# A mixture-of-experts loop whose sums stay in four PSUM banks, with expert weights loaded as half slabs

## The reference, cut to what matters

```
y = zeros(256, 1024)
for each block of tokens that chose the same expert e:
    xb    = the block's tokens
    y_blk = (silu(xb @ w_gate[e]) * (xb @ w_up[e])) @ w_down[e]
    y[token] += weight[token, e] * y_blk
x = x + gt2 * y
```

## Time and profile before

| what | value |
|---|---|
| timed runs, median of 3 | 3115.14 us |
| profiled execution, its own time | 3118.14 us |
| its span, first to last instruction | 3116.3 us |
| mean granted TensorE clock | 0.959 |
| TensorE / VectorE / ScalarE busy | 92% / 63% / 50% of the span |
| the loop over experts | from about 505 to 1379 us of the span |
| DMA in the loop | 345 GB/s mean between 600 and 1300 us |

### The profile page before, as it was taken

The page is one execution under the profiler, slowest core; times in us unless marked ns, Lnnn a source line. Parts: engine busy times, 40 slices in busy tenths (PEclk is TensorE's granted clock), DMA queues, the critical chain, the costliest instruction groups (busy, mean ns, idle before and its releaser), DMA issues.

```text
span 3116.3 us, 42400 instructions
## 1 busy us (share of the span) xinstructions
PE 2864.4 (92%) x15763; PEld 2357.9 (76%) x15763; DVE 1956.5 (63%) x2197; ACT 1550.4 (50%) x1558; POOL 183.6 (6%) x210
## 2 busy tenths in 40 slices
PE   7999998999899998979999999899999999998997
PEld 1476787667676766768898897789788988977996
DVE  1335667888888888874567436544545674375554
ACT  2143455777777777763444434434334454354342
POOL 0000000000000000000045000000000540000000
PEclk9989998999999999998998999999989999999999
DMA  7522436898989989873343005444433420154454
GB/s 301 189 81 81 182 135 257 342 351 332 356 337 361 349 331 348 338 289 115 136 143 128 1 4 220 176 169 175 178 112 136 159 109 1 36 203 160 176 190 169
DMA packets 57945, 612.11 MB, mean 196 GB/s; under 512 B 12641, under 2 KB 18337, under 8 KB 21442
## 3 DMA queue, kind: packets, MB, share of 16 engines
q1 hardware_dynamic: 57794, 610.04, 51.6%
HBM read 608.97 MB, written 1.05 MB: 196 GB/s over the span
## 4 chain that ended last, share of the span: by engine, by line
issue 47%; PE 27%; DVE 10%; DMA 6%; POOL 5%; ACT 4%; DVEq 0%; SPq 0%; POOLq 0%; ACTq 0%
DVE arena_rounded L1608 8%; DMA weight_slabs<-in_expert_slabs 5%; PE psum_vector L572 3%; ACT arena_rounded L1605 3%; PE psum_vector L517 2%; PE psum_vector L519 2%; PE psum_vector L518 2%; POOL arena L3183 2%; PE psum_scalar L517 2%; PE psum_vector L1654 2%; PE psum_scalar L518 2%; PE psum_scalar L519 2%; PE psum_vector L544 2%; POOL arena L3186 2%; PE psum_scalar L1641 2%
## 5 line engine op out<-in xcount | busy, mean ns | idle before, releaser
L2004 DVE TENSOR_TENSOR weight_slabs_rounded<-weight_slabs,arena_rounded 128x2048 fp32r<-128x2048 f32 x208 | 478.1, 2306 | 427.3 <-ACT arena_rounded L2001 410.4
L1608 DVE TENSOR_TENSOR arena_rounded<-weight_slabs,arena_rounded 128x2048 fp32r<-128x2048 f32 x290 | 651.5, 2287 | 64.2 <-ACT arena_rounded L1605 52.0
L2001 ACT ACTIVATE arena_rounded<-weight_slabs 128x2048 fp32r<-128x2048 f32 x208 | 396.1, 1912 | 454.7 <-PE psum_vector L519 261.9
L1605 ACT ACTIVATE arena_rounded<-weight_slabs 128x2048 fp32r<-128x2048 f32 x290 | 548.1, 1912 | 137.9 <-DMA weight_slabs<-in_expert_slabs 57.3
L517 PE MATMUL psum_vector<-arena_rounded,arena_rounded 128*128 128x512 f32 (+3 forms) x1312 | 480.2, 366 | 41.6 <-DVE weight_slabs_rounded L2004 31.0
L517 PE MATMUL psum_scalar<-arena_rounded,arena_rounded 128*128 128x256 f32 (+1 forms) x1456 | 477.8, 328 | 32.0 <-DVE weight_slabs_rounded L2004 17.3
L1641 PE MATMUL psum_scalar<-arena_rounded,arena_rounded 128*128 128x512 f32 x768 | 322.4, 420 | 72.8 <-DVE arena_rounded L1608 62.8
L519 PE MATMUL psum_vector<-arena_rounded,arena_rounded 128*128 128x512 f32 (+3 forms) x960 | 375.5, 391 | 0.0
L518 PE MATMUL psum_vector<-weight_slabs_rounded,arena_rounded 128*128 128x512 f32 x880 | 348.8, 396 | 0.0
L517 PEld LDWEIGHTS psum_scalar<-arena_rounded,arena_rounded 128*128 128x128 f32 x1456 | 285.0, 196 | 62.3 <-issue 12.5
L517 PEld LDWEIGHTS psum_vector<-arena_rounded,arena_rounded 128*128 128x128 f32 (+1 forms) x1312 | 256.6, 196 | 83.4 <-DVE weight_slabs_rounded L2004 41.1
(11 more groups left out here) (462 smaller groups left out, 4212.1 us busy)
## 6 DMA issues: line engine op xcount, KB each, us to landing
weight_slabs<-in_expert_slabs SPq DMA_DIRECT2D x145, 2048.0 KB, 9.2
weight_slabs<-in_layer_slabs SPq DMA_DIRECT2D x103, 2048.0 KB, 7.7
weight_slabs<-in_mixer_slabs SPq DMA_DIRECT2D x32, 2048.0 KB, 7.5
weight_slabs<-in_layer_slabs SPq DMA_DIRECT2D x6, 1024.0 KB, 5.5
arena<-in_mem SPq DMA_DIRECT2D x3, 1024.0 KB, 10.2
arena<-in_b_gate SPq DMA_DIRECT2D x6, 512.0 KB, 4.6
constants<-in_constants SPq DMA_DIRECT2D x1, 1025.0 KB, 5.2
arena<-in_x SPq DMA_DIRECT2D x1, 1024.0 KB, 7.5
```

The source lines that it names most:

```text
L1605: e.activation(high_, whole, ACT.Copy).then_inc(S("expert_high"), 1)
L1608: e.tensor_tensor(low, whole, high_.bitcast(F32), ALU.subtract).then_inc(S("expert_split"), 1)
L2001: e.activation(fr(high), low, ACT.Copy).then_inc(S("weights_high"), 1)
L2004: e.tensor_tensor(fr(low), low, fr(high).bitcast(F32), ALU.subtract).then_inc(S("weights_split"), 1)
```

## The change: what it does

The sums over the experts stay in PSUM: all four banks of `psv` accumulate through the whole loop, two tiles of 128 tokens by two sides of 512 columns. `combine` writes them with `start=False`. Ahead of the loop TensorE writes zeros there (4 fp32 matmuls with a zeroed `selwT`), behind a wait for the first gathered tokens (`xg_ready`). VectorE's `combined` goes, and at the end one instruction multiplies the four banks by `gt2`. The rings are remade: folds, gather and down sums share two banks (`psa` bank 2 and a new one in `pst`), the gate and up sums and the transposes the other two. A block takes 6 banks of the first ring: folds 0 and 1, gather, fold 2, two down sums. Expert slabs are loaded as halves of 1024 KB, each with its own semaphore count, and each as soon as the difference of the half before it in that place is done. GpSimd clears `selwT` earlier and `yacc` no more.

```
-MOE_V, MOE_A, MOE_STEP = 10, 7, 8
+MOE_V, MOE_A, MOE_STEP = 6, 7, 8
...
-        pst = ctx.enter_context(nc.psum_tensor("psum_tick", [P, 2], F32))
+        pst = ctx.enter_context(nc.psum_tensor("psum_tick", [P, BANK], F32))
+        moe_vector_banks, moe_scalar_banks = [psa[:, 2, :], pst[:, :]], [psa[:, 0, :], psa[:, 1, :]]
...
-            G = Banks(pe, psv, moe["vector_full"], moe["vector_free"])
+            G = Banks(pe, moe_vector_banks, moe["vector_full"], moe["vector_free"])
+            pe.wait_ge(m["scalar_free"], MIX_A + 3)
...
+            step(e.memset(selwT, 0.0))
+            e.sem_inc(S("set_for_products"), 1)
             e.wait_ge(S("blocks_known"), 1)
-            for sum_ in (yacc, ye, selwT):
-                step(e.memset(sum_, 0.0))
+            step(e.memset(ye, 0.0))
             e.sem_inc(S("ye_ready"), 1)
...
-                for n in slabs_:
-                    sp.wait_ge(S("expert_split"), 18 * i + 2 * n + 2)
-                    src = a["expert_slabs"][bass.ds(expert, 1), n, :, :].rearrange("e p n -> (e p) n")
-                    sp.dma_start(flat_slab(n % 3), src).then_inc(m[f"slab{n % 3}"], 16)
+                for h in halves_:
+                    sp.wait_ge(S("expert_split"), 18 * i + h + 1)
+                    src = a["expert_slabs"][bass.ds(expert, 1), h // 2, :, :].rearrange("e p n -> (e p) n")
+                    at = h % 2 * 4 * BANK
+                    sp.dma_start(expert_half(h)[0], src[:, at:at + 4 * BANK]).then_inc(half_arrived(h)[0], 16)
...
-            def combine(V):
+            def combine(last=False):
                 for t in range(NT):
-                    for half in range(2):
-                        V.close(pe.matmul(V.open(), selwT[:, t * P:(t + 1) * P], ye[:, half * BANK:(half + 1) * BANK],
-                                          start=True, stop=True))
+                    for side in range(2):
+                        mm = pe.matmul(psv[:, 2 * t + side, :], selwT[:, t * P:(t + 1) * P],
+                                       ye[:, side * BANK:(side + 1) * BANK], start=False, stop=last)
+                return mm
...
+            pe.wait_ge(S("set_for_products"), 2)
+            pe.wait_ge(S("xg_ready"), 1)
+            for bank in range(4):
+                pe.matmul(psv[:, bank, :], selwT[:, 0:P], cst[:, 0:BANK], start=True, stop=False)
             with pe.Fori(0, n_blocks) as i:
-                V = Banks(pe, psv, m["vector_full"], m["vector_free"], base=MOE_V * i + 1, looped=True)
-                A = Banks(pe, psa, m["scalar_full"], m["scalar_free"], base=MOE_A * i, looped=True)
+                V = Banks(pe, moe_vector_banks, m["vector_full"], m["vector_free"], base=MOE_V * i + 1, looped=True)
+                A = Banks(pe, moe_scalar_banks, m["scalar_full"], m["scalar_free"], base=MOE_A * i, looped=True)
...
-                combine(V)
+                combine()
...
-            def combined(V):
-                for t in range(NT):
-                    for half in range(2):
-                        cell = yacc[:, t, half * BANK:(half + 1) * BANK]
-                        V.give(tt(cell, cell, V.take(), ALU.add))
...
                 low_parts(2, 3, 4, 5, 6)
-                combined(V)
                 low_parts(7)
...
-            combined(V)
-            V.given()
             Splitter(e, 0, high=False).upto(1)
             step = Count(e, S("vector_between"))
-            step(tt(yacc, yacc, over(gt2, NT), ALU.mult))
+            e.wait_ge(m["vector_full"], MOE_V * n_blocks + 2)
+            step(tt(yacc, psv[:].rearrange("p (t b) n -> p t (b n)", b=2), over(gt2, NT), ALU.mult))
```

More of the change, by code:

```diff
@@ L191, in __init__ @@
         self.base, self.looped, self.n, self.closed = base, looped, 0, 0
-        self.size = psum.shape[1]
+        self.banks = psum if isinstance(psum, list) else [psum[:, k, :] for k in range(psum.shape[1])]
+        self.size = len(self.banks)
     def open(self, after=None):
@@ L203, in open @@
         self.n += 1
-        return self.psum[:, n % self.size, :]
+        return self.banks[n % self.size]
     def close(self, mm):
@@ L218, in take @@
         self.eng.wait_ge(self.full, self.base + self.n + 1)
-        return self.psum[:, self.n % self.size, :]
+        return self.banks[self.n % self.size]
     def give(self, ins, wait=False):
@@ L824, in pe_mixer @@
             used_now(mm)
[L825 removed]
+            pe.wait_ge(S("set_for_products"), 1)
             for n in range(2):
```

56 lines of the change are left out of this document (29 added, 27 removed).

## The result

The kernel after takes 3120.9 us (median of 20 runs) where the kernel before took 3115.6 us beside it: ratio 1.0018, 95% interval 1.0011 to 1.0025. It is slower, by 3.4 to 7.8 us. The forecast was 3115 us, with "no change" as its likeliest case at 0.48. The time lies in the range of 3096 to 3140, and the direction was missed.

What follows compares the result with a forecast made beforehand. No engine is full; a chain of waits between engines sets 54.55 us a block. Terms -19.0 -1.4 +19.3 +4.35 +0.2 -3.2 = +0.2 us on 3118.14; the median lies 3.0 us lower: 3115 us, range 3096 to 3140.

Steps and rivals of the forecast that it cites:

- no change: Case that the whole kernel's time stays within 0.2% of the median before; chance 0.48.
- The clock (gain): TensorE's wait for difference 7 shrinks to about 1 us, so four blocks' falls to the low clock vanish: -3.2 us.
- the four old falls: Four blocks before the change where TensorE dropped to 1.2 GHz behind its wait for difference 7; priced 3.2 us.
- a rival (0.15): Clock falls at the new pause ahead of product 12, 1.6 us in each of 16 blocks: 3144 us; chance 0.15.
- The ring of two (cost): Product 12 waits for fold 2's bank, so copy 15 starts 1.21 us late in each of 16 blocks: +19.3 us.
- The zeros (cost): Four fp32 matmuls ahead of the loop delay difference 7 of the first block: +4.35 us, bounds 3.6 and 7.2.
- The additions (gain): Without VectorE's additions, difference 7 starts sooner, only as far as copy 7 allows: 19.0 us won in all.
- the half loads (gain): Halves end copy 2's DMA wait, 0.09 us a block: 1.4 us; they land in time, 5.5 us after issue.
- The end: Behind the loop, last additions are hidden by the first layer slab; one multiply reads four PSUM banks: +0.2 us.
- The sum: All gains and costs over the whole kernel: +0.2 us on the profiled execution's 3118.14 us, forecast 3115 us.

Runs made afterwards that it cites:

- e1: Kernel before with only the expert slabs loaded as halves; additions and rings as before: 3091.4 us, ratio 0.9915.
- e4: Kernel after with the second down sum in a free bank of the gate and up sums, so product 12 waits for no multiply: 3094.6 us, 0.9927.
- e8: Kernel after with one unused fp32 matmul of 512 columns per block, filling the pause ahead of product 12: ratio 0.9990 to the kernel before.
- e5: e4 with the choice of slots moved ahead of difference 7, into VectorE's idle time: 3077.0 us, ratio 0.9866 to the kernel before.
- e2: Kernel after with whole slabs of 2048 KB instead of halves, sums still in PSUM: 3131.6 us, ratio 1.0048 to the kernel before.
- e6: e5 with the zeros issued ahead of the wait for the first gathered tokens: 3072.4 us, ratio 0.9857 to the kernel before.
- e9: e1 with the choice of slots moved ahead of difference 7, additions still in the loop: ratio 1.0004 to the kernel before.
- e12: e9 with two unused fp32 matmuls of 512 columns per block between products 6 and 7: ratio 0.9939 to the kernel before.
- e3: Kernel before with one added TensorE wait ahead of product 12, for the multiply of fold 2: 3149.4 us, ratio 1.0104.
- e10: e2 with the second down sum in the free bank, as in e4: ratio 0.9975 to the kernel before.
- e11: Kernel before with two unused fp32 matmuls (512 and 256 columns) per block between products 6 and 7: ratio 0.9999.
- e7: e1 with the added wait of e3 ahead of product 12, no sums kept in PSUM: ratio 0.9998 to the kernel before.

## Why the prediction was wrong, step by step

- **The clock (gain), the step that failed.** The prediction counted the four old falls as gone and no new ones: -3.2 us. The old ones did go: behind product 6 none is left, and e1, with the same short pause there, has no fall in 15 periods. But the change makes a new pause of 1.10 us ahead of product 12, and three blocks fell behind it, 1.45 us each: +4.3 us. The prediction had this as a rival (0.15), priced it about right for a block (1.6 us), but for all 16 blocks, and gave it nothing in the sum. What belonged into the sum was a share of them: before, pauses of 1.4 to 2.5 us were followed by a fall in 4 of 15 blocks, and the same share of 16 blocks at 1.6 us would have been 6.8 us (an estimate from these numbers). That would have made the forecast "slower". e4 and e8 show the cause: without the pause, and with the pause filled, there are no falls.
- **The ring of two (cost).** The mechanism was right, the place too (TensorE idle, released by the multiply, product 12 late, nothing behind it takes it up). The term was 1.21 us and measured 1.31: 21.0 instead of 19.3. Its two parts were read less well than their sum. Product 12 is 1.29 us late (6.62 - 5.33), not 1.0: the hop from the multiply to product 12 is 0.23 us (657.90 + 0.42 to 658.55), not the 0.05 that was assumed, and before product 12 started at 926.92, ahead of the 927.11 that was taken. The other 0.2 us, for a product that starts after a wait, is not there: from product 12 to copy 15 it is 2.14 us after and 2.13 before. The two errors cancel in part, which is luck. That the first down sum has to wait for the gather's bank was not listed; the wait for fold 2's bank hides it here, and it costs 0.1 us in e4. e4 takes the main wait away: its span is 24.3 us under that of the kernel after, of which 19.2 are the wait (8.76 - 7.56, 16 times) and 4.3 its falls.
- **The zeros (cost).** 4.35 expected, 2.8 measured: the clock rose at about 508 us, sooner than in the trace of before. e5's execution, in which it rose late, had 4.3. Either value can come.
- **The additions (gain)** and **the half loads (gain).** 19.0 and 1.4 expected, 19.0 and 1.3 measured. That the additions would give no more than copy 7 allows was right to 0.01 us. What the prediction did not say: the halves alone give the same 19 us (e1), and so do the sums in PSUM alone (e2), so the second of the two adds nothing. As the gain was counted only once, the sum is right; a reader who took the accumulation for the cause of the gain would have been wrong. The halves landed after 7.0 us, not 5.5, still in time. The 5.5 us were not "latency for the most part" either: at the 345 GB/s of the loop 1024 KB take 3.0 us of them (an estimate from the two rows).
- **The end.** +0.2 expected. The layer slab landed in 7.57 us instead of 8.24, which no run sets apart from noise.
- **The sum.** +0.2 expected. The measured terms give +4.8: 4.3 from the falls and 1.7 from the ring above the forecast, 1.5 from the zeros below it. The falls are the largest: without them the sum would be +0.5, which these runs could not tell from no change. The prediction took 6.2 us for the least that a measurement can tell; with 20 runs of each kernel the interval was 4.4 us wide, and a difference of 5.3 us stood clear of zero.

The Trainium skill's rule that the prediction weighed ("TensorE: Matmul & The Clock Gate", "A second HAM failure mode: psum-queue depth-cycling") was right in kind: frequent short idling between groups of matmuls lets the clock swing. The traces agree and add a number: 3 blocks behind 1.10 us of it, 11 of 15 behind 2.07 us, none where it is filled. What the Trainium skill has against halves did not bind: the 1 MiB that "DMA: Bandwidth & Descriptors", "Rules for kernel authors", asks for is just met by 1024 KB, and the window of the loop in e6 shows the rate (us; busy us and count of PE, PEld, DVE, ACT, POOL; clock; DMA share; GB/s):

```profile
600.00:1300.00 700.00, 648.54 (x3128) 496.41 (x3127) 615.70 (x445) 539.66 (x445) 0.00 (x0) 1.00 0.94 364
```

Transfers of 1024 KB ran at a mean of 364 GB/s there, queued behind each other, without one wait of ScalarE for a half. The 341 GB/s that the same page of the Trainium skill gives for 1 MB ("Bandwidth") is no ceiling for such a queue; the measurement decides.

## What to carry to other kernels

When a ring of PSUM banks shrinks, list for each opening the reader that must give the bank back and what stands ahead of that reader in its queue: here one opening cost 1.3 us in every block, another 0.5 to 2.0 us where a slab was late (falls of the clock included), and a third 0.1 us. Taking work off an engine that idles anyway brings nothing until other work of that engine is moved into the hole: the sums in PSUM were worth 0 us a block in the change as made and 1.3 us with the choice of slots moved (51.94 against 53.20), and the kernel with all of it (e6) beats the kernel before by 1.4%, that after by 1.6%. A pause of TensorE is to be priced with its share of falls of the clock. Where the pause can't be removed, as it was in e4, a matmul without use in it can be the cheapest repair.

## What was unexpected of the hardware

- Matmuls without use paid: 1.8 us of them in each block made e9 0.65% faster (e12), 0.9 us made the kernel after 0.28% faster (e8; the traces account for half of it), in both cases with no change in what TensorE waits for.
- A fall cost 0.3 to 2.0 us of a period in the kernel before, 1.4 to 1.5 in the kernel after, and 1.5 to 3.2 in e9. Pauses of equal length (2.05 and 2.07 us in e9) were followed by a fall or not.
- Where the pause stands matters. Ahead of product 3, between products of 512 columns, TensorE idles 1.20 to 1.27 us in every block of e1 and of the kernel after, and no fall followed; falls came there only behind 1.84 to 2.38 us (e3, e10, e11). The pause of 1.10 us ahead of product 12, behind the folds and the gather (64 columns), was followed by one in 3 blocks of the kernel after and 3 of e2, and that of 1.19 us in 3 (e7) and 6 (e3). Why the second place is worse was not tried apart: the matmuls ahead of the pause differ, and so does the idling shortly before.
